# A two-block transformer kernel: VectorE's order in the attention stage, four weight splits, and the feed-forward halves changed

## The reference

```python
proj = rmsnorm(h) @ w_in                  # u, q, k, v, g_ssm, g_att
y_ssm = s5_mixer(u, ...)                  # complex diagonal recurrence, 32 groups of 64 states
q, k = rmsnorm per head; o = diff_attention(q, k, v, lam, slopes)   # 4 heads, two softmaxes each
mixed = sigmoid(g_ssm) * (y_ssm @ w_ssm_out) + sigmoid(g_att) * (y_att @ w_att_out)
h = h + mixed @ w_o
up = rmsnorm(h) @ w_up; a, b = up[..., :2816], up[..., 2816:]
h = h + (gelu(causal_conv3(a)) * b) @ w_down
```

## Time and profile before

| what | value |
|---|---|
| median of 3 runs | 740.59 us |
| profiled execution, in all | 744.92 us |
| its span | 743.1 us |
| TensorE (PE) busy | 709.0 us, 95% |
| VectorE (DVE) busy | 537.3 us, 72% |
| ScalarE (ACT) busy | 379.9 us, 51% |
| mean granted TensorE clock | 0.991 of full |
| longest pauses of TensorE | 3.14 at 251.7, 2.90 at 113.8, 2.84 at 125.4, 2.04 at 532.0, 2.04 at 10.8, 1.60 at 207.8 |

### The profile page before, as it was taken

The page is one execution under the profiler, slowest core; times in us unless marked ns, Lnnn a source line. Parts: engine busy times, 40 slices in busy tenths (PEclk is TensorE's granted clock), DMA queues, the critical chain, the costliest instruction groups (busy, mean ns, idle before and its releaser), DMA issues.

```text
span 743.1 us, 14560 instructions
## 1 busy us (share of the span) xinstructions
PE 709.0 (95%) x6152; PEld 665.5 (90%) x6152; DVE 537.3 (72%) x954; ACT 379.9 (51%) x564; POOL 23.9 (3%) x50
## 2 busy tenths in 40 slices
PE   6999997999989899999999999999889999999996
PEld 4988996888989899999999999888888989989995
DVE  5898669657878767777777799966867656556553
ACT  6577456448356343444443684478554344343441
POOL 3010000000000000000000150000000000000000
PEclk9999999999999999999999999999999999999999
DMA  7751243115445455555555554424245556556541
GB/s 239 213 161 59 67 162 115 59 59 158 144 153 174 154 184 172 189 204 174 174 197 197 177 171 131 153 80 132 84 162 167 201 173 208 186 187 210 174 167 56
DMA packets 94700, 115.66 MB, mean 156 GB/s; under 512 B 7971, under 2 KB 83932, under 8 KB 94636
## 3 DMA queue, kind: packets, MB, share of 16 engines
q1 hardware_dynamic: 94244, 114.51, 47.2%
q0 software_dynamic: 128, 0.13, 0.1%
q10 hardware_dynamic: 264, 0.10, 0.1%
HBM read 113.69 MB, written 1.05 MB: 154 GB/s over the span
## 4 chain that ended last, share of the span: by engine, by line
PE 78%; DVE 11%; ACT 6%; issue 3%; DMA 1%; SPq 0%; DVEq 0%; ACTq 0%
PE psum L1761 17%; PE psum L1762 16%; PE psum L1763 16%; PE psum L2299 4%; PE psum L2298 4%; PE psum L2297 4%; DVE w_lo L1060 3%; PE psum L2069 3%; PE psum L2067 3%; PE psum L2065 3%; ACT w_hi L492 2%; PE psum L1873 1%; PE psum L1908 1%; DMA xtok<-in_x_dram 1%; PE psum L2122 1%
## 5 line engine op out<-in xcount | busy, mean ns | idle before, releaser
L1060 DVE TENSOR_TENSOR w_lo<-w_raw,w_hi 128x2048 fp32r<-128x2048 f32 x105 | 240.0, 2288 | 101.0 <-ACT w_hi L492 100.7
L492 ACT ACTIVATE w_hi<-w_raw 128x2048 fp32r<-128x2048 f32 x105 | 199.8, 1907 | 58.4 <-PE psum L2299 34.5
L1761 PE MATMUL psum<-x2n_hi,w_hi 128*128 128x256 f32 x400 | 113.3, 283 | 2.1 <-DVE w_lo L1060 1.2
L1762 PE MATMUL psum<-x2n_lo,w_hi 128*128 128x256 f32 x400 | 110.9, 277 | 0.0
L1763 PE MATMUL psum<-x2n_hi,w_lo 128*128 128x256 f32 x400 | 110.8, 277 | 0.0
L1761 PE MATMUL psum<-hs_hi,w_hi 128*128 128x256 f32 (+1 forms) x352 | 100.3, 285 | 3.1 <-DVE ff L979 3.1
L1762 PE MATMUL psum<-hs_lo,w_hi 128*128 128x256 f32 (+1 forms) x352 | 99.9, 284 | 0.0
L1763 PE MATMUL psum<-hs_hi,w_lo 128*128 128x256 f32 (+1 forms) x352 | 99.8, 283 | 0.0
L1761 PEld LDWEIGHTS psum<-x2n_hi,w_hi 128*128 128x128 f32 x400 | 75.1, 188 | 5.1 <-DVE w_lo L1060 1.4
L1762 PEld LDWEIGHTS psum<-x2n_lo,w_hi 128*128 128x128 f32 x400 | 75.2, 188 | 0.7
L1763 PEld LDWEIGHTS psum<-x2n_hi,w_lo 128*128 128x128 f32 x400 | 75.3, 188 | 0.0
(11 more groups left out here) (438 smaller groups left out, 1516.9 us busy)
## 6 DMA issues: line engine op xcount, KB each, us to landing
w_raw<-in_w_ff_dram SPq DMA_DIRECT2D x32, 1024.0 KB, 5.3
w_raw<-in_w_in_dram SPq DMA_DIRECT2D x27, 1024.0 KB, 5.3
w_raw<-in_w_up_dram SPq DMA_DIRECT2D x22, 1024.0 KB, 5.1
w_raw<-in_w_down_dram SPq DMA_DIRECT2D x11, 1024.0 KB, 5.0
w_raw<-in_w_o_dram SPq DMA_DIRECT2D x4, 1024.0 KB, 5.1
w_raw<-in_w_out_dram SPq DMA_DIRECT2D x4, 1024.0 KB, 5.2
w_raw<-in_w_ssm_out_dram SPq DMA_DIRECT2D x2, 1024.0 KB, 5.2
w_raw<-in_w_att_out_dram SPq DMA_DIRECT2D x2, 1024.0 KB, 5.1
```

The source lines that it names most:

```text
L492: A.activation(w_hi[:, u % NW, :], raw[:, u % NRAW, :], ACT.Copy).then_inc(sem("hi_ready"), 1)
L1060: V.tensor_tensor(w_lo[:, u % NRAW, :], raw[:, u % NRAW, :], w_hi[:, u % NW, :].bitcast(F32), ALU.subtract).then_inc(sem("lo_ready"), 1)
L1761: T.matmul(out_, lh, rh, start=start, stop=False)
L1762: T.matmul(out_, lh, rl, start=False, stop=False)
```

## The change

It has these parts. Nothing of what is computed is changed.

1. VectorE's `split_to(5)` moves from behind the four B products to between the second and the third.
2. ScalarE's `split_to(8)` moves from before the squares of q and k to behind the root `qk_rms`.
3. On VectorE the first scan pair moves to just behind `s5_mults(1)`, its four products (`s5_back`) around gate 0, the C products among the gate groups, `split_to(12)` ahead of `c_sums`, a gate group ahead of `mix_a(1)`, and the second scan pair ahead of `mix_b(1)`.
4. ScalarE makes the high half of w_o 0 (unit 21) right behind that of att_out 1, before the mix copies. VectorE's `split_to(19)` moves from before the reciprocal of `rs2` to between the two groups of `evac_ssm(0)`.
5. The feed-forward passes 0 to 9 run up_b before up_a, in the order of weights too; the last keeps up_a first. ScalarE copies up_b into a new buffer `ub`, and VectorE multiplies from there. The exponentials and the logarithm move from the last pass to the one before.
6. Five buffers of the second block's feed-forward part lie 64 bytes higher, and it shares the semaphore `ff`.

Cut to the changed lines and those beside them:

```diff
@@ -79,6 +79,13 @@
+def up_order(i):
+    if i >= KF // 2:
+        return ()
+    return ("up_b", "up_a") if i < KF // 2 - 1 else ("up_a", "up_b")
@@ -107,9 +114,9 @@
     for i in range(KF // 2 + 1):
-        if i < KF // 2:
-            add(("up_a", i), w_up[:, :, 256 * i:256 * i + 256], 8, "feat", 2)
-            add(("up_b", i), w_up[:, :, FF + 256 * i:FF + 256 * i + 256], 8, "feat", 2)
+        for name in up_order(i):
+            c0 = 256 * i + (FF if name == "up_b" else 0)
+            add((name, i), w_up[:, :, c0:c0 + 256], 8, "feat", 2)
         if i:
@@ -251,6 +258,7 @@
 ff = sb("ff", [P, 2, 2, 256], F32, k(A0 + 16384))
+ub = sb("ub", [P, 2, 2, 256], F32, k(81664))
 x2 = sb("x2", [P, KD, 256], F32, k(25664))
@@ -291,11 +299,11 @@
 uu = sb("uu", [P, 2, 2, 256], F32, k(54400))
-u_hi = sb("u_hi", [P, 2, 2, 256], F32R, k(58496))
-u_lo = sb("u_lo", [P, 2, 2, 256], F32R, k(62592))
-outb = sb("outb", [P, 2, D], F32, k(66688))
-nf = sb("nf", [P, D], F32, k(74880))
-sqj = sb("sqj", [P, 2, 512], F32, k(78976))
+u_hi = sb("u_hi", [P, 2, 2, 256], F32R, k(58560))
+u_lo = sb("u_lo", [P, 2, 2, 256], F32R, k(62656))
+outb = sb("outb", [P, 2, D], F32, k(66752))
+nf = sb("nf", [P, D], F32, k(74944))
+sqj = sb("sqj", [P, 2, 512], F32, k(79040))
@@ -602,13 +610,13 @@
     split_to(7)
-    split_to(8)
     act.wait_ge(sem("C_ready"), 4)
...
     A.activation(rs[:, :], banks[3][:, 0:TOK], ACT.Sqrt, scale=1.0 / 64).then_inc(sem("qk_rms"), 1)
+    split_to(8)
     split_to(9)
@@ -737,10 +745,8 @@
         A.activation(yatt_hi[:, h, :], oT[:, h, T0:TOK], ACT.Copy).then_inc(sem("yatt_hi"), 1)
-    split_to(21)
+    split_to(unit_at[("w_o", 0)]["n"] + 1)
     for m in range(8):
-        if m == 4:
-            split_to(unit_at[("att_out", 1)]["n"] + 2)
         act.wait_ge(sem("mixed"), m + 1)
@@ -750,23 +756,38 @@
         A.activation(sq[:, m % 2, 0:NQ], hT[:, m, T0:TOK], ACT.Square).then_inc(sem("h1_sq"), 1)
-    split_to(unit_at[("up_a", 0)]["n"] + 2)
+    split_to(unit_at[("up_b", 0)]["n"] + 2)
     act.wait_ge(sem("h1_stat"), 1)
     A.activation(rstd[:, :], banks[3][:, 0:NQ], ACT.Sqrt, bias=eps_col, scale=1.0 / D).then_inc(sem("h1_rms"), 1)
-    for i in range(KF // 2):
-        split_to(unit_at[("up_a", i)]["n"] + 3)
+    def gelu_a(i):
         for m in range(2):
...
             A.activation(gl[:, i % 2, m, :], cv_[:, i % 2, m, :], ACT.Gelu_apprx_tanh).then_inc(sem("gl"), 1)
-        split_to(unit_at[("up_b", i)]["n"] + 3)
-        if i == KF // 2 - 1:
+    def copy_up_b(i):
+        evac("up_b", i, lambda m, b: A.activation(ub[:, i % 2, m, :], b[:, 0:256], ACT.Copy))
+    for i in range(KF // 2):
+        first, second = up_order(i)
+        split_to(unit_at[(first, i)]["n"] + 3)
+        if first == "up_b":
+            copy_up_b(i)
+        else:
+            gelu_a(i)
+        split_to(unit_at[(second, i)]["n"] + 3)
+        if second == "up_b":
+            copy_up_b(i)
+        else:
+            gelu_a(i)
+        if i == KF // 2 - 2:
             act.wait_ge(sem("tiny_v"), 1)
...
         for m in range(2):
-            taken(act, group(("up_b", i), m))
+            act.wait_ge(sem("ff"), 2 * i + m + 1)
             if i >= 2:
@@ -1072,9 +1093,9 @@
-    def scaled(name, i, dst, c0):
+    def scaled(name, i, dst, c0, ms=(0, 1)):
         u = unit_at[(name, i)]
-        for m in range(2):
+        for m in ms:
             g = u["g0"] + m
@@ -1128,7 +1149,8 @@
         (mark if i < 3 else seq)(i_)
-    split_to(5)
+        if i == 1:
+            split_to(5)
     for part, op in ((0, ALU.subtract), (1, ALU.add)):
@@ -1185,14 +1207,17 @@
-    def c_products():
+    c_made = []
+    def c_products(tiles):
         dve.wait_ge(sem("s5_copied"), 4 * CH + 10)
-        for i, (part, f) in enumerate(((0, 0), (1, 1), (1, 0), (0, 1))):
-            i_ = tt(c_prod[:, i], c_cmp[:, part][:, None, :, :].to_broadcast([P, 3, NS, 16]),
-                    l_pow[:, f][:, :, :, None].to_broadcast([P, 3, NS, 16]), ALU.mult)
-            (mark if i < 3 else seq)(i_)
+        for i in tiles:
+            part, f = ((0, 0), (1, 1), (1, 0), (0, 1))[i]
+            c_made.append(mark(tt(c_prod[:, i], c_cmp[:, part][:, None, :, :].to_broadcast([P, 3, NS, 16]),
+                                  l_pow[:, f][:, :, :, None].to_broadcast([P, 3, NS, 16]), ALU.mult)))
     def c_sums():
+        dve.wait_ge(sem("dve_seq"), c_made[3])
         tt(c_prod[:, 0], c_prod[:, 0], c_prod[:, 1], ALU.add).then_inc(sem("s5_weights"), 1)
@@ -1218,15 +1243,23 @@
+    scanned = {}
...
         mark(V.tensor_tensor_scan(sz[:, 1, h], flat(mag_t, h), sz[:, 0, h], 0.0, ALU.mult, ALU.add))
-        seq(V.tensor_tensor_scan(sz[:, 3, h], flat(mag_t, h), sz[:, 2, h], 0.0, ALU.mult, ALU.add))
+        scanned[h] = mark(V.tensor_tensor_scan(sz[:, 3, h], flat(mag_t, h), sz[:, 2, h], 0.0, ALU.mult,
+                                               ALU.add))
+    def s5_back(h, part):
         c, s = flat(Ec, h), flat(Es, h)
-        mark(tt(sz[:, 0, h], sz[:, 1, h], c, ALU.mult))
-        seq(tt(sz[:, 2, h], sz[:, 1, h], s, ALU.mult))
-        seq(V.scalar_tensor_tensor(out=sz[:, 1, h], in0=sz[:, 3, h], scalar=-1.0, in1=s, op0=ALU.mult,
-                                   op1=ALU.mult))
-        tt(sz[:, 3, h], sz[:, 3, h], c, ALU.mult).then_inc(sem("s5_n"), 1)
+        dve.wait_ge(sem("dve_seq"), scanned[h])
+        if part == 0:
+            mark(tt(sz[:, 0, h], sz[:, 1, h], c, ALU.mult))
+            scanned[h] = mark(tt(sz[:, 2, h], sz[:, 1, h], s, ALU.mult))
+        else:
+            seq(V.scalar_tensor_tensor(out=sz[:, 1, h], in0=sz[:, 3, h], scalar=-1.0, in1=s, op0=ALU.mult,
+                                       op1=ALU.mult))
+            tt(sz[:, 3, h], sz[:, 3, h], c, ALU.mult).then_inc(sem("s5_n"), 1)
@@ -1304,28 +1337,39 @@
-    gates = lambda i: scaled("gate", i, gate, T0)
+    def gates(i, ms=(0, 1)):
+        scaled("gate", i, gate, T0, ms)
+    s5_scan(0)
     max_a(0)
     max_b(0)
-    gates(0)
+    s5_back(0, 0)
+    gates(0, (0,))
+    s5_back(0, 1)
+    c_products((0,))
+    gates(0, (1,))
     split_to(11)
     mix_a(0)
-    gates(1)
+    gates(1, (0,))
+    c_products((1, 2))
+    gates(1, (1,))
     mix_b(0)
-    c_products()
+    c_products((3,))
     max_a(1)
+    split_to(12)
     c_sums()
-    split_to(12)
     gates(2)
     split_to(13)
+    gates(3, (0,))
     mix_a(1)
-    s5_scan(0)
-    gates(3)
+    gates(3, (1,))
     max_b(1)
...
     split_to(14)
+    s5_scan(1)
     mix_b(1)
-    s5_scan(1)
+    s5_back(1, 0)
+    s5_back(1, 1)
     s5_y(0)
@@ -1356,7 +1400,6 @@
     gates(7)
-    split_to(19)
     dve.wait_ge(sem("o_rms"), 1)
@@ -1373,7 +1416,9 @@
-    evac_ssm(0, (0, 1))
+    evac_ssm(0, (0,))
+    split_to(19)
+    evac_ssm(0, (1,))
@@ -1451,8 +1496,9 @@
     for i in range(KF // 2):
-        ua, ub = unit_at[("up_a", i)], unit_at[("up_b", i)]
-        split_to(ua["n"] + 3)
+        first, second = up_order(i)
+        ua = unit_at[("up_a", i)]
+        split_to(unit_at[(first, i)]["n"] + 3)
         for m in range(2):
@@ -1465,18 +1511,16 @@
                                    op0=ALU.mult, op1=ALU.add).then_inc(sem("conv"), 1)
-        split_to(ub["n"] + 3)
+        split_to(unit_at[(second, i)]["n"] + 3)
         for m in range(2):
...
         for m in range(2):
-            j, g = 2 * i + m, ub["g0"] + m
-            dve.wait_ge(sem("group_done"), g + 1)
-            tt(ff[:, i % 2, m, :], gl[:, i % 2, m, :], banks[g % NB][:, 0:256], ALU.mult).then_inc(
-                sem(f"group_free{g % NB}"), 1)
+            taken(dve, group(("up_b", i), m))
+            tt(ff[:, i % 2, m, :], gl[:, i % 2, m, :], ub[:, i % 2, m, :], ALU.mult).then_inc(sem("ff"), 1)
         for m in range(2):
-            taken(dve, group(("up_b", i), m))
+            dve.wait_ge(sem("ff"), 2 * i + m + 1)
             dve.wait_ge(sem("ff_hi"), 2 * i + m + 1)
@@ -1735,9 +1779,9 @@
             r = relu[:, i % 2, m, :]
-            tt(uu[:, i % 2, m, :], r, r, ALU.mult).then_inc(sem("uu"), 1)
+            tt(uu[:, i % 2, m, :], r, r, ALU.mult).then_inc(sem("ff"), 1)
         for m in range(2):
-            dve.wait_ge(sem("uu"), 2 * i + m + 1)
+            dve.wait_ge(sem("ff"), KF + 2 * i + m + 1)
             dve.wait_ge(sem("u_hi"), 2 * i + m + 1)
@@ -2074,9 +2118,10 @@
     for i in range(KF // 2):
-        unit("up_a", i, (hs_hi, hs_lo, 0, NQ), 8, ready=None if i else "hs_lo",
-             between=None if i else h1_stat)
-        unit("up_b", i, (hs_hi, hs_lo, 2, NQ), 8)
+        for name in up_order(i):
+            unit(name, i, (hs_hi, hs_lo, 0 if name == "up_a" else 2, NQ), 8,
+                 ready="hs_lo" if i == 0 and name == "up_b" else None,
+                 between=h1_stat if i == 0 and name == "up_b" else None)
         if i:
```

## The result

The changed kernel takes 735.94 us at the median of 4 runs (735.27 to 736.02), the kernel before 741.16 us in the runs beside it (739.98 to 742.5): a ratio of 0.9926, 95% interval 0.9899 to 0.9953. It is faster by 5.2 us. Forecast were 10.9 us less and 729.7 us (725.0 to 735.5), so the time lies just outside the range and the gain is about half of the forecast (0.48). The profiled execution fell from 743.1 to 734.1 us of span, by 9.0 us.

The account below looks back on a forecast made before the run. TensorE, busy 95% of the span, bounds the kernel; only its waits and low clock can be won. 0 + 0.35 + 7.4 + 0.45 + 4.8 - 2.1 = 10.9 us off the 740.6 median: 729.7 us (725 to 735.5).

Parts of the forecast that it names:

- its gap moved on: TensorE's 1.01 us gap at 41.9 closes; the gap at the BT transposes, 50.4, grows from 0.4 to 1.4 us.
- the four buffers' limit: Squares of q and k: only four buffers hold the eight squares; gain put at 0.35 us, bounds 0 and two squares.
- the half at 109.2: Low half of gate 3 ready at 109.2 instead of 113.7, wanted at 110.9, so TensorE's 2.90 us wait closes.
- `turn_a(1)` without a pause: TensorE reaches `turn_a(1)` at 119.7, `max_b(1)` is ready at 119.3, so the 2.84 us wait goes.
- 2.90 + 2.84 + 1.7: Attention stage: waits before gate 3 and in `turn_a(1)`, plus low clock from 126 to 130 us, sum 7.4 us.
- the new gap: In ssm_out 1 TensorE waits 1.5 us for a bank, as `split_to(19)` delays VectorE's gate evacuation.
- full gain of 1.9: Mixing stage: upper bound of the gain put at 0.45 us, bounds 0 and 1.9.
- +4.8 and -2.1: Feed-forward: start gains 3.14 us of bank wait plus 1.7 of clock; backlog at the last pass costs 2.1.
- The wait of down 10: Last feed-forward pass: TensorE waits 0.6 us for `ff_lo` before down 10.
- the same 10.9 off either: Whole kernel: 10.9 us taken off both the profiled 744.9 us, giving 734.0, and the median 740.6, giving 729.7.
- Rival 2: Freed time only partly kept, through small slack or a clock that falls anyhow: 3 to 4 us less, 733.5; chance 0.20.
- Rivals 1, 3 and 4: Two backlogs absent, 726.1 (0.15); weights' arrival replaces the waits, 740 (0.03); feed-forward passes slip past their slack, 747 (0.04).

Follow-up runs that it names:

- e14: Kernel before with only the new order of scans, C products, `split_to(12)` and gate groups, one more execution: 735.56 us profiled.
- e9: Changed kernel with the five shifted buffers back at their old addresses: 736.41 us, ratio 0.9897 to the kernel before.
- e13: Kernel before, unchanged, one more execution: 744.01 us profiled.
- e2: Kernel before with only the 64-byte shift of the five buffers: 741.72 us, ratio 0.9996.
- e3: Kernel before with only the new order of scans, C products, `split_to(12)` and gate groups: 738.0 us, ratio 0.993.

## Why the prediction was right or wrong

**The bound, and edits 1 and 2.** What the edits won is pauses and slow clock, as said. The time moves by the pace of the matmuls too, which this bound leaves out. From TensorE's second unit to the start of A all nineteen profiles take 69.29 to 69.35 us, with and without these edits. Edit 1 was worth 0 as said, and its gap moved on, in two parts: 0.46 and 1.05, 1.5 together, forecast 1.4 in one. Edit 2 was put at 0.35 and is 0: the four buffers' limit, my lower bound, was the right one. ScalarE makes four squares early and then waits 1.67 us until TensorE has read the first, so the last square ends no sooner, and TensorE has its new gap of 0.50 us in between:

```profile
65.24 1.39 ACT L616 ACTIVATE sqk<-qkT 128x272 f32<-128x272 f32 x4 [1.67 <-PE psum L1979]
```

**Edit 3, 7.4 forecast, 6.06 measured** (7.58 against the one profiled execution). The order of work, the half at 109.2 and `turn_a(1)` without a pause came true. The step that failed is "2.90 + 2.84 + 1.7": it adds a pause and a slow stretch as if every execution had both. In five of the six executions without the edit the clock fell with the first pause (to 0.66 to 0.79 on the mean from 110 to 118 us), work at that clock took the place of at least 1.5 of the second pause's 2.84 us, and the clock was back at 1.00 before the point that VectorE sets. So the low clock cost nothing of its own there, and the term is mis-sized by 1.3. The Trainium skill ("TensorE: Matmul & The Clock Gate", section "Why this matters for your kernels") says that a pause between bursts of matmuls takes the clock down. Five of the six traces agree at the pause of 2.90 us; the one that I had read agrees only at its second.

**Edit 4, 0.45 forecast, 0.4 measured**, with its two halves: the new gap 1.19 (forecast 1.5) in ssm_out 1, and the full gain of 1.9 (B 41.2 to 39.3) when it is taken away again, the bound I had given.

**Edit 5, +4.8 and -2.1 forecast, +5.2 and -2.35 measured** between the profiled executions (C 52.48 to 47.25, D 111.69 to 114.05). The clock's part of the gain is there only where the clock falls: against e14 it is 3.7, between my bounds of 3.1 and 4.8. The wait of down 10 is 0.72 for 0.6, and the moved turn shows the backlog to be VectorE's lateness at the last pass. The copies took 8.2 us of ScalarE for the forecast 10.4 and cost nothing on the path: P1 is 17.06 with and without them. The Trainium skill ("VectorE: DVE Perf Modes", section "Rules for kernel authors") names the copy out of PSUM for the case that many operations follow. Here one follows and the copy pays, since it is made by ScalarE and frees the bank for which TensorE waited.

**Edit 6, 0 forecast.** It is the one part where nothing in the rows of before could be read. It makes no difference to the median of the kernel before (ratio 0.9996), and a difference to the changed kernel isn't shown (e9). In the profiles P2 is 11.10 with it for 10.96 or 11.17, and the shorter P1 stands only in profiles with it.

**The sum against the profile.** From the profiled execution of before to the one after the stretches change by -7.60 - 0.37 - 5.23 + 2.36 = -10.8 us, forecast -10.9. The rest up to the -9.0 of the spans lies in parts that the change doesn't touch: the passes of the second feed-forward part +1.7 (from the first to the end of the last, 164.7 to 166.4), TensorE's first unit +0.5 (it takes 8.2 to 9.3 us over all profiles), and -0.4 in the first pass and the norm. With these 1.8 us the profiled 734.0 of the forecast would have been 735.8; it is 735.9 in all. That this sum comes out to 0.1 us is in part luck: errors of its terms cancel (edit 2 0.35 too much, edit 5's gain 0.4 too little), and the profile read was the rare one with A = 76.32. From e13, a more usual execution of before, the same stretches fall by 9.2 us.

**The sum against the median: the step that failed.** I wrote that the profiled execution lay 4.3 us above the median and took "the same 10.9 off either", as if 4.3 were an offset that both kernels share. It isn't: the profiled execution belongs to the upper heap of before, and of the three runs behind the median two belong to the lower, while of the changed kernel all four runs, the profiled one among them, lay within 0.8 us at its upper end. So the profiled execution is 4.3 us above the median before and level with it after, and the gain at the median is smaller by about that much (5.2 for 9.0 between the profiled ones). The size of the 4.3 fits the pace; as said under e2 that is inferred and not seen. Mean against mean the difference is 8.0 us, and the stretches of a usual execution give 6.06 + 0.4 + 5.2 - 2.35 - 1.7 = 7.6. So of the 10.9, 3.3 us were not there to win on the mean: 1.3 of edit 3's term, 0.35 of edit 2, and 1.7 of the second feed-forward part, which was put at nothing. The rest up to the 5.2 of the first result is the draw of four runs against four. Rival 2, 733.5 by freed time only partly kept, was nearest in number and wrong in kind: the clock stayed at 1.00 and no wait came back in edit 3's stretch. Rivals 1, 3 and 4 show in no profile.

## What to carry to other kernels

- Before a sum is taken off a median, look whether the profiled execution is typical of the runs: compare a stretch that no edit touches (here one pass of a long loop) over several executions. A forecast for few runs needs a range as wide as their spread, here 8 us.
- A pause and the slow clock behind it don't add up when a second wait follows: find the point that the other engine sets, and count up to that. Here the slow clock ahead of that point cost nothing, the one behind it 1.5 us.
- A reordering that helps the first pass of a loop and hurts its last should be turned back in the middle, where slack works the lateness off: at 17.06 us a pass the turn was free after two or four passes, cost a bank wait of 2.1 us after one, and 2.35 us at the last. It holds only as far as there is slack: at 16.67 us a pass VectorE gained 0.18 us a pass, and 1.1 to 1.7 us were left at the end.

## What the runs showed of the hardware that I had not expected

- Back-to-back matmuls of one shape (128x128 with 256 columns, float32), at a granted clock of 1.00 and without a gap, start 113.5 to 113.9 ns apart on the mean in some executions and 117.8 in others. The value holds through 100 to 170 us of work, differs between executions of one kernel (the changed one, 16.67 or 17.06 us a pass), and can be the one in the first feed-forward part and the other in the second (e2: 113.5, then 117.8). What sets it stays open; the profiles hint at ties to edit 6 and to edit 3, and no run was made that decides.
- With the moving operand's buffer 64 bytes higher the mean of the 128x512 matmul was 389 ns instead of 392 (before) or 394 (e3), and all nine profiles had the same one of the three values of P2.
- Past the same pause of 2.90 us the clock was full in one execution (1.00 from 110 to 118 us) and at the lower level for a while in five (0.66 to 0.79 on the mean of that stretch). The pause of 3.03 to 3.14 us at the start of the feed-forward part was followed by a full clock in one execution of six (e14).
